# The turn from the first output projection to the first feed-forward: three up tiles per input tile, squares summed on VectorE, the norm's column sums beside the fourth tile

## What is computed

```python
mixed = (sigmoid(g_a) * y_a + sigmoid(g_b) * y_b) @ w_out          # "wout" in the kernel
h = h + rms_norm(mixed, norm_gains[1])                              # norm 1
xn = rms_norm(h, norm_gains[2])                                     # norm 2
u = causal_depthwise_conv(xn @ w_up, conv_w, conv_b)                # "up": 1024 x 5632
u_gate, u_val = split(u, 2)
ffn = (gelu(u_gate) * u_val) @ w_down                               # "down"

def rms_norm(x, g):
    return x * rsqrt(mean(x * x, axis=-1) + EPS) * g
```

## Time and profile before

| | |
|---|---|
| median of 3 runs | 1641.21 us (1638.36 to 1643.59) |
| the profiled execution's own time | 1640.41 us |
| its span | 1638.6 us |
| granted PE clock, mean over the span | 0.969 of full |
| PE busy | 1542.1 us (94% of the span) |
| DVE busy | 1024.6 us (63%) |
| ACT busy | 645.1 us (39%) |
| POOL busy | 25.3 us (2%) |

### The profile page before, as it was taken

One profiled execution on the slowest core, in us unless ns is written; L12 is line 12 of the kernel. 1 busy time (PEld: TensorE's weight loads), 2 busy tenths in 40 slices (PEclk: granted clock), 3 DMA queues, 4 the chain that ended last, 5 costly groups with the idle time before them and its releaser, 6 DMA issues. The chain is left out here.

```text
span 1638.6 us, 25916 instructions
## 1 busy us (share of the span) xinstructions
PE 1542.1 (94%) x10792; PEld 1375.9 (84%) x10792; DVE 1024.6 (63%) x1430; ACT 645.1 (39%) x1031; POOL 25.3 (2%) x22
## 2 busy tenths in 40 slices
PE   7999999999997999999999899999876999999996
PEld 7989778878997999999888687767565999998885
DVE  4533345775445777777665666685565888885454
ACT  4423442333223221212343445545543555554342
POOL 0000000000000000000000011000000000000000
PEclk9999998999998999999999899999998999999998
DMA  4221004352330233332444203110102132222322
GB/s 172 78 89 66 14 21 148 123 165 74 103 104 33 99 128 104 122 110 91 129 149 153 101 30 103 52 39 21 39 26 90 57 125 103 104 104 69 99 91 77
DMA packets 37268, 147.62 MB, mean 90 GB/s; under 512 B 4256, under 2 KB 4384, under 8 KB 27296
## 3 DMA queue, kind: packets, MB, share of 16 engines
q1 hardware_dynamic: 37008, 144.92, 26.6%
q0 software_dynamic: 144, 1.05, 0.2%
HBM read 143.86 MB, written 2.10 MB: 89 GB/s over the span
## 5 line engine op out<-in xcount | busy, mean ns | idle before, releaser
L528 PE MATMUL ps<-t 128*128 128x258 f32 (+4 forms) x2144 | 687.9, 321 | 36.5 <-DVE t L2085 11.4
L530 PE MATMUL ps<-t 128*128 128x258 f32 (+4 forms) x2144 | 678.0, 316 | 0.0
L529 PE MATMUL ps<-t 128*128 128x258 f32 (+4 forms) x2144 | 676.3, 315 | 0.0
L528 PEld LDWEIGHTS ps<-t 128*128 128x128 f32 (+1 forms) x2144 | 411.1, 192 | 76.3 <-issue 26.5
L529 PEld LDWEIGHTS ps<-t 128*128 128x128 f32 (+1 forms) x2144 | 411.2, 192 | 24.7 <-issue 0.2
L530 PEld LDWEIGHTS ps<-t 128*128 128x128 f32 (+1 forms) x2144 | 410.0, 191 | 26.0
L2042 DVE TENSOR_TENSOR t<-t 128x2048 fp32r<-128x2048 f32 (+2 forms) x123 | 210.4, 1710 | 227.8 <-ACT t L1400 227.8
L1400 ACT ACTIVATE t<-t 128x2048 fp32r<-128x2048 f32 (+2 forms) x123 | 177.7, 1445 | 181.0 <-PE ps L530 174.2
L1369 PE MATMUL ps<-t 128*128 128x256 f32 x532 | 150.6, 283 | 0.0
L1367 PE MATMUL ps<-t 128*128 128x256 f32 x532 | 150.3, 282 | 0.0
L1368 PE MATMUL ps<-t 128*128 128x256 f32 x532 | 149.1, 280 | 0.0
(11 more groups left out here) (296 smaller groups left out, 1846.3 us busy)
## 6 DMA issues: line engine op xcount, KB each, us to landing
t<-in_W SPq DMA_DIRECT2D x76, 1024.0 KB, 4.9
t<-in_W SPq DMA_DIRECT2D x62, 512.0 KB, 3.6
t<-in_W SPq DMA_DIRECT2D x96, 256.0 KB, 3.8
t<-in_W SPq DMA_DIRECT2D x4, 644.0 KB, 3.9
t<-in_XT SPq DMA_DIRECT2D x8, 264.0 KB, 6.7
out<-t SPq DMA_DIRECT2D x8, 256.0 KB, 2.1
t<-in_ROPE POOLq DMA_DIRECT2D x1, 1024.0 KB, 7.2
t<-in_CONS SPq DMA_DIRECT2D x1, 423.0 KB, 7.8
```

The costliest lines, as they stand in the source:

```text
L528: pe.matmul(out, wh, xh, start=first, stop=False)
L529: pe.matmul(out, wh, xl, start=False, stop=False)
L530: return pe.matmul(out, wl, xh, start=False, stop=last)
```

## The change

It does five things.

1. Norm 1: ACT squares the last tile straight from PSUM, before it copies it; that square isn't added by DVE, but summed by PE by itself, behind the sum of the other seven (`DIRECT[1] = (7,)`).
2. Chunk ("up", 1) is converted ahead of the tile loop: on ACT before `eps(1)`, on DVE behind a wait for POOL's power of norm 1. The conversion of ("up", 2) takes the place behind the loop, and DVE's loop over pairs converts from i = 2 on.
3. PE's loop over the input tiles computes three up tiles, 0, 1 and 2, so 18 matmuls for each input tile.
4. Norm 2: DVE adds the squares of tiles 0 to 5 into `tmp[1]` (five more L2051 instructions, inside its loop), PE sums that once behind tile 6, and the squares 6 and 7 each by itself behind the loop (`DIRECT[2] = (6, 7)`).
5. Up tile 3 is computed behind these sums, its first half ahead of the norm's spread and its second behind it. The spread goes to free columns of banks 0 to 3 and the sums to free columns of bank 7; ACT copies the spread out in two pieces.

```diff
-NORM_BY_PE = (False, False, True, False, True, False, False)
+DIRECT = ((), (7,), (6, 7), (), tuple(range(8)), (), ())
...
+        def norm_acc(i):
+            return (tmp[1] if i in (2, 4) else rst)[:, 0:NORM_N[i]]
...
             pe.wait_ge(S["ev_y"], 16)
             norm_sums(1, 4)
+            norm_sum_of(1, 4, 7)
             norm_spread(1, 4)
-            for c in range(22):
+            w = weights(AT["up", 0], 8)
+            pe.wait_ge(S["ev_wo_a"], 4)
+            pe.wait_ge(S["ev_wo_d"], 4)
+            pe.wait_ge(S["rst"], 2)
+            for k in range(8):
+                pe.wait_ge(S["xl"], 17 + k)
+                for z in range(3):
+                    x = w if z < 2 else weights(AT["up", 1], 8)
+                    for q in range(2):
+                        cols, a = slice(128 * (z % 2), 128 * (z % 2) + 128), q * HQ[0]
+                        ins = three(bank(2 * z + q, HQ[q]), x[0][:, k, cols], x[1][:, k, cols],
+                                    x2h[:, k, a:a + HQ[q]], x2l[:, k, a:a + HQ[q]], k == 0, k == 7)
+                    if k == 7:
+                        ins.then_inc(S["mm_up"], 1)
+                if k == 6:
+                    norm_sums(2, 7, 264)
+            w = weights(AT["up", 1], 8)
+            norm_sum_of(2, 7, 6, 264)
+            norm_sum_of(2, 7, 7, 264)
+            for q in range(2):
+                for k in range(8):
+                    ins = three(bank(6 + q, HQ[q]), w[0][:, k, 128:256], w[1][:, k, 128:256],
+                                x2h[:, k, q * HQ[0]:q * HQ[0] + HQ[q]], x2l[:, k, q * HQ[0]:q * HQ[0] + HQ[q]], k == 0, k == 7)
+                if q == 0:
+                    pe.wait_ge(S["pow"], 3)
+                    for j, (a, m) in enumerate(col_tiles(TQ)):
+                        sp = pe.matmul(bank(min(j, 3), m, off=264 if j < 4 else 392), rcol[:, j:j + 1].to_broadcast([P, P]),
+                                       C("id")[:, 128 - m:128], start=True, stop=True, skip_group_check=True)
+                    sp.then_inc(S["spr"], 1)
+            ins.then_inc(S["mm_up"], 1)
+            for c in range(2, 22):
                 w = weights(AT["up", c], 8)
-                if c == 0:
-                    pe.wait_ge(S["ev_wo_a"], 4)
-                    pe.wait_ge(S["ev_wo_d"], 4)
-                    for k in range(8):
-                        pe.wait_ge(S["xl"], 17 + k)
-                        for z, b in enumerate((0, 2)):
...
-                        norm_sum_of(2, 6, k)
-                    norm_spread(2, 6)
-                    continue
                 for i in range(2):
                     j = 2 * c + i
-                    if j == 3:
-                        pe.wait_ge(S["rst"], 3)
-                    if j >= 4:
-                        pe.wait_ge(S["up_c"], j - 3)
+                    pe.wait_ge(S["up_c"], j - 3)
...
# ScalarE
                     j = 2 * c + i
+                    if j == 7:
+                        ac.wait_ge(S["mm_wout"], j + 1)
+                        square(1, j, pair(2, TQ // 2), True)
                     if j % 2:
...
-                    square(1, j, mo[:, j, 0:TQ])
+                    if j < 7:
+                        square(1, j, mo[:, j, 0:TQ])
+            split(AT["up", 1])
             eps(1, 4)
             spread(1, 4)
-            ac.wait_ge(S["sum"], SUM0[2])
+            ac.activation(shr[:, :, 0], modc[:, 0:8], ACT.Copy).then_inc(S["cst"], 1)
             for k in range(8):
                 ac.wait_ge(S["rs_b"], k + 1)
                 ac.activation(x2h[:, k, :], h[:, k, Q0:T1], ACT.Copy, scale=V("g2", k)).then_inc(S["xh"], 1)
                 square(2, k, h[:, k, Q0:T1])
-            split(AT["up", 1])
-            ac.activation(shr[:, :, 0], modc[:, 0:8], ACT.Copy).then_inc(S["cst"], 1)
-            eps(2, 6)
-            spread(2, 6)
+            split(AT["up", 2])
+            eps(2, 7, 264)
+            ac.wait_ge(S["spr"], 3)
+            ac.activation(rst[:, 0:512].rearrange("p (b n) -> p b n", b=4), ps[:, 0:4, 264:392], ACT.Copy)
+            ac.activation(rst[:, 512:TQ], bank(3, TQ - 512, off=392), ACT.Copy).then_inc(S["rst"], 1)
...
             for i in range(22):
-                if i > 0:
+                if i > 1:
                     split(AT["up", i] + 1)
...
# VectorE
-            add(1, 7)
...
+            dv.wait_ge(S["pow"], 2)
+            split(AT["up", 1])
             dv.wait_ge(S["rst"], 2)
             for k in range(8):
...
                 if k >= 1:
                     x2_low(k - 1)
+                if 2 <= k <= 6:
+                    add(2, k - 1)
             x2_low(7)
-            split(AT["up", 1])
+            split(AT["up", 2])
...
-                if part == 0 and i > 0:
+                if part == 0 and i > 1:
                     split(AT["up", i] + 1)
```

More of the change, by code:

```diff
@@ L167 @@
 NORM_N = (T1, TQ, TQ, T2, T2, T2, T2)
-NORM_BY_PE = (False, False, True, False, True, False, False)
-SUM0 = [sum(0 if NORM_BY_PE[j] else 7 for j in range(i)) for i in range(8)]
-COL0 = [sum(8 if NORM_BY_PE[j] else 1 for j in range(i)) for i in range(8)]
+DIRECT = ((), (7,), (6, 7), (), tuple(range(8)), (), ())
+SUM0 = [sum(max(7 - len(d), 0) for d in DIRECT[:i]) for i in range(8)]
+COL0 = [sum(min(len(d) + 1, 8) for d in DIRECT[:i]) for i in range(8)]
 XS0 = (0, None, 8, 16)
@@ L567, in tokens, with col_stat @@
                 return ins
-            def col_stat(src, n, b, first, rhs):
+            def col_stat(src, n, b, first, rhs, off=0):
                 for j, (a, _) in enumerate(col_tiles(n)):
-                    ins = pe.matmul(bank(b, 1, off=j), src[:, a:a + 128], rhs, start=(first and j == 0), stop=True,
+                    ins = pe.matmul(bank(b, 1, off=off + j), src[:, a:a + 128], rhs, start=(first and j == 0), stop=True,
                                     skip_group_check=True)
@@ L1419, in eps @@
                 ac.wait_ge(S["col"], COL0[i + 1])
-                ac.activation(rcol[:, 0:nc_], bank(b, nc_), ACT.Identity, bias=con[:, a:z]).then_inc(S["eps"], 1)
+                ac.activation(rcol[:, 0:nc_], bank(b, nc_, off=off), ACT.Identity, bias=con[:, a:z]).then_inc(S["eps"], 1)
             def spread(i, b):
@@ L2050, in add @@
                 dv.wait_ge(S["sq"], 8 * i + k + 1)
-                dv.tensor_tensor(rst[:, 0:n], rst[:, 0:n], sq[k % 2][:, 0:n], ALU.add).then_inc(S["sum"], 1)
+                dv.tensor_tensor(norm_acc(i), norm_acc(i), sq[k % 2][:, 0:n], ALU.add).then_inc(S["sum"], 1)
             def norm_tiles(a, norm, n, src, gain, shift, xh, xl, k0=0, k1=8):
```

38 lines of the change are left out of this document (18 added, 20 removed).

## The result

| | before | changed |
|---|---|---|
| median of 20 runs each | 1637.01 us (1628.55 to 1647.96) | 1629.03 us (1623.86 to 1634.37) |
| ratio of changed to before | | 0.9959 (95%: 0.9941 to 0.9977) |
| profiled execution | 1640.41 us, span 1638.6 | 1626.85 us, span 1625.0 |
| granted clock, mean over the span | 0.969 | 0.974 |

The change makes the kernel faster, by 0.2 to 0.6% in this series: some 7 us (the three runs of before that stood ahead of the prediction are among its twenty). Two things make the difference, and they are kept apart here: the gain of the change, and the level from which it was counted.

The account below looks back on a forecast made before the run. PE bounds the up stage; 9.2 us gained if PE alone counted, 6.9 after DVE's late conversion, less 1.7 for clock, is 5.2. From 1640.4 this gives 1635.2, put at 1635.5 us, range 1632.0 to 1639.0.

Parts of the forecast that it names:

- The level: Whole kernel: starting time for the gain, from the profiled 1640.41 us; changed median put between two readings, at 1635.5 us.
- the rival with the right mechanism: Stop ahead of up tile 6 costs no clock, or DVE's pairs are faster: gain 6.9 to 8 us, chance 0.22.
- The clock in the stop: Behind PE's stop ahead of up tile 6 the clock falls to half, losing 1.7 us of the 6.9 gained.
- The eight of ten: The trace's ten PE stops of 2.0 to 2.7 us: behind eight of them the granted clock falls to half.
- Norm 1: Norm 1's end: the last square read from PSUM and summed by PE lets DVE start its first tile 1.4 us earlier.
- The additions in DVE's turns: Input-tile loop: five additions make DVE's turns 2.69 us but cost nothing, filling what was wait for PE.
- The clock in the loop: Input-tile loop: PE's new waits of 0.5 us a tile leave it at full clock.
- The rival "falls in the loop and stays down": Input-tile loop: PE at half clock needs 4.3 us a tile, up tile 6 15 us later, 1655.4 us; chance 0.04.
- Norm 2's end: Behind the loop: power hidden by up tile 3, spread at full clock, DVE takes up tile 0 0.3 us later than before.
- Who is late next: Ahead of up tile 6: PE stops 2.3 us for DVE's conversion of chunk ("up", 3); 6.9 us gained, no second stop.
- The rival that DVE's lag weighs more: DVE's sequence up to tile 6: power or additions slow it 0.2 to 0.4 us a turn; gain 1.5 to 4, chance 0.25.
- The column sums side by side: Behind input tile 7: PE's two more sums take 2.15 us, at full clock.

Follow-up runs that it names:

- same_again: The changed kernel once more, unaltered, beside the kernel before on the same chip; 1629.8 us, ratio 0.9933 to before.
- norm1_added: Changed kernel with norm 1 as before: ACT copies wout tile 7 and squares the copy, DVE adds all eight squares; 1626.7 us, ratio 0.9928 to before.
- eps_first: Changed kernel with ACT's conversion of chunk 1 moved from ahead of norm 1's eps to behind it; 1625.7 us, ratio 0.9924 to before.
- squares_by_pe: Changed kernel with all eight squares of norm 2 summed by PE, no additions on DVE, three up tiles in the loop; 1638.1 us, ratio 1.0011 to before.
- sums_apart: Changed kernel with PE's sum of square 6 moved between up tiles 0 and 1 of input tile 7; 1629.2 us, ratio 0.9931 to before.
- power_first_alone: Changed kernel, only DVE's conversion of chunk 2 waits for POOL's power of norm 2; one run, up tile 15 ends at 118.82 us, no total given.
- experiments 10 and 11: Changed kernel plus 3.1 us useless PE work behind the two sums: three column sums (10) or 26 matmuls (11); up tile 15 ends at 125.17 and 121.92 us.
- two_tiles: Changed kernel with two up tiles in the input loop, tiles 2 and 3 behind it, spread inside tile 2; 1632.5 us, ratio 0.9939 to before.
- spread_first: Changed kernel with norm 2's spread ahead of up tile 3 instead of in its middle; 1630.1 us, ratio 0.9941 to before.
- column_sums_longer: Changed kernel with three more, useless one-column sums (30 instructions) behind the two sums; one run, up tile 15 ends at 125.17 us, no total given.

## Why the prediction was wrong, point by point

Two terms failed: the level from which the gain was counted, 3.7 us too high, and the loss of clock taken for the stop ahead of up tile 6, 1.7 us where the runs show none. The order of events in the stage came as forecast.

**The level: wrong, and most of the miss.** "So I put the median of the changed kernel between the two readings, at 1635.5 us" started from one execution of 1640.4 and three runs of 1641.2. With the gain of 5.2 that is a level of 1640.7. Twenty runs have 1637.0, 3.7 lower. That profile's clock, 0.969, was there to be read, and ten stops of PE that may or may not lose clock were in the sum's own text, but only for one stop was their chance turned into time. The spread of the runs, 1628 to 1654 for one kernel, goes, by the correlation of -0.98, nearly all with the clock. Neither my number nor my range had a term for it, and the range, 7 us wide, had to hold the gain's uncertainty alone. With the right level the number would have been 1631.8, 2.8 above the measured: of the miss of 6.5, 3.7 is the level and 2.8 the gain. Even the rival with the right mechanism, 1632.4 to 1633.5, lies above the 1629.0, by the level.

**The clock in the stop: wrong.** "Behind eight of them the granted clock falls to half ... I take it: 6.9 - 1.7 = 5.2." The term of 1.7 us measured nothing: the clock fell behind none of the nine stops of about 2.0 us ahead of tile 6 (changed kernel, same_again, norm1_added, eps_first, squares_by_pe, sums_apart, power_first_alone and the two kernels with useless work). The rival without that loss (6.9 to 8 us, chance 0.22) is what happened: 7.2. The eight of ten were a mixture. Among them are stops beside column sums and small matmuls, where PE's work counted for little already, and these nine lie between long runs of full matmuls, as do the two of the ten that kept the clock. That this is the difference wasn't tried by itself and isn't shown; experiments 10 and 11 speak for it.

**Norm 1: right.** Forecast 1.4 us, measured 1.6, with the conversion ahead of eps costing 0.73 to 0.85 of it (eps_first). The spread ran at half clock, as taken. Undoing this part gave 1.60 back.

**The additions in DVE's turns: right in the timeline, under-priced as an edit.** Turns of 2.67 us (516.33 to 519.00), PE waiting nearly nothing (7.96 of 8.00 busy), the loop no longer than before. But "they fill what was wait for PE" is half of it. With the sums on PE and three tiles a turn the loop stays at half clock for 15.5 us; there the edit is worth 11.1 us, where the work alone would be some 5.

**The clock in the loop: right.** The rival "falls in the loop and stays down" (0.04) didn't happen in the changed kernel, nor in two_tiles, where PE waits 0.94 to 0.98 us in every turn. The loss that the Trainium skill describes for loops that wait for their next tile ("TensorE: Matmul & The Clock Gate", section "HAM oscillation") isn't in these traces for waits of this length. The loop of that section waits for a DMA in every turn, longer than the some 2 us that it computes, so this prediction's waits of 0.5 us are another case. (The rival whose sum that place points to is the third, not the second.) Half clock without waits is what the loop with one-column sums, squares_by_pe, had.

**Norm 2's end: right, 0.5 too late.** Forecast 0.3 later than before, measured 0.2 earlier (in same_again 0.06 later). The power took 2.07, between the ends 1.17 and 2.65, and was hidden, as power_first_alone shows. The end of it 1.0 us behind the conversion was forecast at 0.87 by the earlier trace rows.

**Who is late next: right.** A stop ahead of tile 6, by DVE's conversion of chunk 3, forecast 2.3 us at 556.6, measured 2.01 at 555.6; no second stop. It goes when the conversion comes a pair earlier, and it absorbs changes of TensorE's work ahead of it (two_tiles, spread_first). The rival that DVE's lag weighs more (0.25) fell: DVE's durations stood as they were.

**The column sums side by side: missed.** The sum put two of them behind tile 7 at full clock, and nothing behind them. In four of nine profiles with the two sums side by side and no stop behind them it fell, at some 1.5 us. The changed kernel's own two profiles didn't have it, and that is luck: the same TensorE program in eps_first did.

**The chances.** Faster had 0.52, and came: the ratio 0.9959 is beyond 0.3%, though the upper end of its interval, 0.9977, isn't. One outcome doesn't tell whether 0.52 was too low. The gain itself, 7.2 us in the stage against 5.2, is within the 2 to 8.5 that the unknown costs gave.

## What to carry to other kernels

Read how far single runs of the kernel spread, and the clock of the profiled one, before taking it as the level; a forecast of time needs a term for it even where the change doesn't touch it. When work is pulled ahead on the engine that bounds the kernel, look for the next thing that this engine needs from a helper: moving that one conversion a pair forward gave another 2.2 us, and until then the stop took up about half of what was added to TensorE's work ahead of it (two_tiles, spread_first). Keep one-column matmuls on TensorE few, not many in a row, and out of places where the clock has to rise.

## What the runs showed of the hardware that I had not expected

- TensorE's clock can fall, and can stay down, while the engine is busy without a gap, where what it does is one-column matmuls. In column_sums_longer it fell 4.9 us into five sums in a row (50 instructions, 6.15 us), and was at half for 7 us; behind two in a row it was at half for 3.4 us in four of nine profiles; with 26 matmuls of 258 columns in place of three of the five sums it didn't fall. In a loop of 18 matmuls and one sum, entered at half clock, it took 15.5 us to rise; without the sum 3.0 to 6.2 us in fourteen profiles. A loop already at full clock kept it with a sum in each turn (before, from 519.3 to 538). What decides between the four and the five stays open here.
- A GpSimd instruction of 128x5 elements that starts beside a VectorE conversion of 128x2048 (two SBUF inputs) ends 1.0 us behind the conversion's end, wherever it began: 2.07, 2.79 and 3.12 us long when it started 1.25, 0.5 and 0.2 us into it, and 1.17 without it. It seems to do nothing until the conversion is nearly over; on 128x4 elements, in before, it ended 0.87 behind. The Trainium skill ("GPSIMD Engine Reference", Specifications) has the SBUF interfaces shared with VectorE, with contention for instructions with two SBUF inputs; the runs agree, and give its size for this pair of instructions.
- Of the difference between executions of this kernel, nearly all goes with the granted clock (correlation -0.98 over 86 runs).
